# Attention's inverse row sums: spread into the bank of the head outputs, one query tile later

## What is computed

```
o = lax.map(q_block, (qn_b, qr_b, jnp.arange(n_blk)))   # 8 query tiles of 128, 8 heads
  sc = (q_nope . k_nope + q_rope . k_rope) * scale       # block-causal mask, CHUNK = 64
  p  = softmax(sc)
  out = p @ v                                            # 64 columns per head
```

## Time and profile before

| | us |
|---|---|
| median of three executions | 1252.3 |
| lowest, highest | 1246.91, 1253.53 |
| the profiled execution | 1250.46 |
| its span in the profile | 1248.4 |
| attention in it, window 106 to 300.5 | 194.5, of which TensorE busy 184.10, VectorE 127.11, ScalarE 115.39 |

### The profile page before, as it was taken

How to read it: one execution, slowest core, us unless ns; L and a number is a source line. 1 busy time by engine, 2 the same in 40 slices (tenths; PEclk the granted TensorE clock), 3 DMA queues, 4 the chain that set the end, 5 groups by cost and what they waited for, 6 DMA issues and landing times.

```text
span 1248.4 us, 18136 instructions
## 1 busy us (share of the span) xinstructions
PE 1108.9 (89%) x6835; PEld 963.9 (77%) x6835; DVE 712.3 (57%) x832; ACT 564.8 (45%) x756; POOL 327.0 (26%) x276
## 2 busy tenths in 40 slices
PE   3998999999999899999998999329999999999940
PEld 3885888888877788888887888329999999999930
DVE  5874666666055711111114232558888888888838
ACT  5334655655144200000003221407888888888823
POOL 3103222212332223333220000122444444444210
PEclk9988999999999999999999999659999999999975
DMA  7010000021204111111113322537999999999737
GB/s 244 1 28 11 7 7 7 7 69 34 52 1 111 34 34 51 49 37 50 51 51 104 105 75 77 212 121 300 394 368 356 341 348 356 363 379 358 284 141 288
DMA packets 93131, 184.27 MB, mean 148 GB/s; under 512 B 29712, under 2 KB 67088, under 8 KB 79248
## 3 DMA queue, kind: packets, MB, share of 16 engines
q1 hardware_dynamic: 82704, 166.65, 38.4%
q0 software_dynamic: 10368, 16.80, 3.6%
HBM read 177.12 MB, written 27.26 MB: 164 GB/s over the span
## 4 chain that ended last, share of the span: by engine, by line
PE 78%; DVE 11%; ACT 4%; issue 2%; DMA 2%; SPq 1%; POOL 0%; ACTq 0%; POOLq 0%; DVEq 0%
PE ps L369 24%; PE ps L371 23%; PE ps L370 23%; PE ps L858 3%; PE ps L658 2%; DVE pt_lo L1319 1%; PE ps L818 1%; DVE negm L1274 1%; SPq L348 1%; DVE q_tmp L1265 1%; ACT prob L987 1%; DVE acc L1600 1%; DVE res L1610 1%; DVE acc L1601 1%; PE ps L667 1%
## 5 line engine op out<-in xcount | busy, mean ns | idle before, releaser
L1554 DVE TENSOR_TENSOR we_lo<-raw_e,we_hi 128x2048 fp32r<-128x2048 f32 x108 | 246.9, 2288 | 48.3 <-ACT we_hi L1096 48.3
L1096 ACT ACTIVATE we_hi<-raw_e 128x2048 fp32r<-128x2048 f32 x108 | 206.1, 1908 | 8.3 <-DMA raw_e<-in_w_exp_gate_dram 3.7
L369 PE MATMUL ps<-ht_hi,w_hi 128*128 128x512 f32 x448 | 176.4, 394 | 0.4 <-DVE ht_lo L1192 0.4
L371 PE MATMUL ps<-ht_hi,w_lo 128*128 128x512 f32 x448 | 174.7, 390 | 0.0
L370 PE MATMUL ps<-ht_lo,w_hi 128*128 128x512 f32 x448 | 174.6, 390 | 0.0
L369 PE MATMUL ps<-we_hi,xst_hi 128*128 128x256 f32 x576 | 169.4, 294 | 0.0
L370 PE MATMUL ps<-we_lo,xst_hi 128*128 128x256 f32 x576 | 163.5, 284 | 0.0
L371 PE MATMUL ps<-we_hi,xst_lo 128*128 128x256 f32 x576 | 163.4, 284 | 0.0
L363 POOL CAST w_hi<-raw 128x1024 fp32r<-128x1024 f32 x36 | 40.7, 1130 | 302.2 <-PE ps L371 270.3
L369 PEld LDWEIGHTS ps<-we_hi,xst_hi 128*128 128x128 f32 x576 | 111.4, 193 | 0.0
L370 PEld LDWEIGHTS ps<-we_lo,xst_hi 128*128 128x128 f32 x576 | 111.1, 193 | 0.0
(11 more groups left out here) (284 smaller groups left out, 2472.8 us busy)
## 6 DMA issues: line engine op xcount, KB each, us to landing
raw_e<-in_w_exp_gate_dram SPq DMA_DIRECT2D x36, 1024.0 KB, 8.6
raw_e<-in_w_exp_up_dram SPq DMA_DIRECT2D x36, 1024.0 KB, 7.9
raw_e<-in_w_exp_down_dram SPq DMA_DIRECT2D x36, 1024.0 KB, 8.7
raw<-in_w_in_dram SPq DMA_DIRECT2D x27, 512.0 KB, 3.8
yin<-y_dram SPq DMA_DIRECT2D x16, 512.0 KB, 6.6
xin<-in_x_dram SPq DMA_DIRECT2D x8, 512.0 KB, 7.2
raw<-in_w_out_dram SPq DMA_DIRECT2D x8, 512.0 KB, 4.1
xre<-in_x_dram SPq DMA_DIRECT2D x8, 512.0 KB, 4.2
```

The costliest lines, as they stand in the source:

```text
L369: pe.matmul(dst, st[0], mv[0], start=first, stop=False)
L371: return pe.matmul(dst, st[1], mv[0], start=False, stop=last)
L1096: act.activation(we_hi[c % 4][:, :], raw_e[c % 6][:, :], ACT.Copy).then_inc(sem("w_hi_ready"), 1)
L1554: dve.tensor_tensor(we_lo[c % 4][:, :], raw_e[c % 6][:, :], we_hi[c % 4][:, :].bitcast(F32), ALU.subtract).then_inc(sem("w_lo_ready"), 1)
```

## The change

`spread_sums(g)` leaves the rotation and writes bank 6, the bank in which `values` gathers the outputs. Banks 4 and 5 are left to the chunks of probabilities, and the table, `bank_of` and `bank_free` go. In the loop the spread stands one step later, between `scores(s + 2)` and `prob_transposes(s)` of steps 5, 9, 13 and so on, and waits until ScalarE has copied bank 6 (`o_copied`). VectorE's `outputs` moves from the end of a fourth step to the start of the next one, ahead of its `row_max`. `values` of the next group now waits for `o_ready`, VectorE's multiplication, where it waited for `o_copied`. After the loop the last spread follows `values(63)` as before, with the new wait.

```diff
-PASSES = []
-for _s in range(NQ):
-    PASSES += [(0, _c) for _c in range(chunks_through(_s - 1) if _s else 0, chunks_through(_s))]
-    if _s % 4 == 0 and _s:
-        PASSES.append((1, _s // 4 - 1))
-PASSES.append((1, NQ // 4 - 1))
-PASS_OF = {_x: _n for _n, _x in enumerate(PASSES)}
...
-        def bank_of(kind, n):
-            return 4 + PASS_OF[kind, n] % 2
...
-                def bank_free(kind, n):
-
-                    if PASS_OF[kind, n] >= 2:
-                        was, m = PASSES[PASS_OF[kind, n] - 2]
-                        pe.wait_ge(sem("o_ready" if was else "pt_lo_ready"), m + 1)
...
-                        bank_free(0, c0 + c)
+                        if c0 + c >= 2:
+                            pe.wait_ge(sem("pt_lo_ready"), c0 + c - 1)
...
                 def spread_sums(g):
 
                     pe.wait_ge(sem("rl_ready"), g + 1)
-                    bank_free(1, g)
+                    pe.wait_ge(sem("o_copied"), g + 1)
                     for i in range(4):
-                        mm = pe.transpose(ps[:, bank_of(1, g), i * P:(i + 1) * P],
+                        mm = pe.transpose(ps[:, 6, i * P:(i + 1) * P],
...
                     if s and s % 4 == 0:
-                        pe.wait_ge(sem("o_copied"), s // 4)
+                        pe.wait_ge(sem("o_ready"), s // 4)
...
                 for s in range(NQ):
                     if s + 2 < NQ:
                         scores(s + 2)
+                    if s % 4 == 1 and s > 1:
+                        spread_sums(s // 4 - 1)
                     prob_transposes(s)
                     if s:
                         values(s - 1)
-                        if s % 4 == 0:
-                            spread_sums(s // 4 - 1)
...
                     if (s + 1) % 4 == 3:
                         inverse_sums((s + 1) // 4)
+                    if s % 4 == 1 and s > 1:
+                        outputs(s // 4 - 1)
                     if s + 2 < NQ:
                         row_max(s + 2)
...
-                    if s % 4 == 0 and s:
-                        outputs(s // 4 - 1)
                     if i < 4 and h + 1 < HEADS:
                         job_read(h + 1, i)
```

More of the change, by code:

```diff
@@ L655, in prob_transposes @@
                     for c in range(i // 4 + 1):
-                        bank_free(0, c0 + c)
+                        if c0 + c >= 2:
+                            pe.wait_ge(sem("pt_lo_ready"), c0 + c - 1)
                         for j in range(4 * c, min(4 * c + 4, i + 1)):
-                            mm = pe.transpose(ps[:, bank_of(0, c0 + c), (j % 4) * P:(j % 4) * P + P],
+                            mm = pe.transpose(ps[:, 4 + (c0 + c) % 2, (j % 4) * P:(j % 4) * P + P],
                                               prob[s % 2][:, j * P:(j + 1) * P], ident[:, :])
@@ L1012, in _ @@
                             act.wait_ge(sem("pv_done"), used + 1)
-                        act.activation(pt_hi[cc % 4][:, 0:w, :].rearrange("p a b -> p (a b)"), ps[:, bank_of(0, cc), 0:w * P],
+                        act.activation(pt_hi[cc % 4][:, 0:w, :].rearrange("p a b -> p (a b)"), ps[:, 4 + cc % 2, 0:w * P],
                                        ACT.Copy).then_inc(sem("pt_hi_ready"), 1)
@@ L1288, in outputs @@
                     dve.wait_ge(sem("sums_spread"), g + 1)
-                    dve.tensor_tensor(o, ps[r:r + VH, bank_of(1, g), :], o, ALU.mult).then_inc(sem("o_ready"), 1)
+                    dve.tensor_tensor(o, ps[r:r + VH, 6, :], o, ALU.mult).then_inc(sem("o_ready"), 1)
                 for t in range(1, NT, 2):
@@ L1318, in _ @@
                         dve.wait_ge(sem("pt_hi_ready"), cc + 1)
-                        dve.tensor_tensor(pt_lo[cc % 4][:, 0:w, :].rearrange("p a b -> p (a b)"), ps[:, bank_of(0, cc), 0:w * P],
+                        dve.tensor_tensor(pt_lo[cc % 4][:, 0:w, :].rearrange("p a b -> p (a b)"), ps[:, 4 + cc % 2, 0:w * P],
                                           pt_hi[cc % 4][:, 0:w, :].rearrange("p a b -> p (a b)").bitcast(F32), ALU.subtract).then_inc(sem("pt_lo_ready"), 1)
-                    if s % 4 == 0 and s:
-                        outputs(s // 4 - 1)
                     if i < 4 and h + 1 < HEADS:
```

## The result

Thirteen executions of each kernel on one chip gave a median of 1254.34 us with the change and 1250.87 us before it. The measured ratio is 1.0035, with a 95% interval of 1.0018 to 1.0052: the change makes the kernel 2.3 to 6.5 us longer (the two medians are 3.5 us apart). The forecast was 4.9 us longer and 1257 us. The median of 1254.34 us lies inside the range, and the cause was named; the size of one term was off. Of the 2.9 us between 1257.2 and 1254.34, 1.4 us come from the kernel before, whose median over thirteen executions is 1250.87 us and not the 1252.3 us of the three on which the forecast was put.

What follows compares the result with a forecast made beforehand. TensorE, 78% of the chain, was taken to bound the kernel. Head places 3.2, last head place 1.12 and end 0.93, less 0.3 at half-head places, made 4.9 us longer: 1257 us from the 1252.3 median, range 1250 to 1262.

Steps and rivals of the forecast that it cites:

- Half-head places: Eight places: the spread's removed 5.4 us of waits worth about nothing, as the next row maximum starts at the same moment.
- Even and odd heads: Half-head places: row maximum overlaps the multiplication by 0.07 us in even heads, nothing taken in odd; 0.3 us gained.
- some 11 us in all: Forecast total of the values' fifteen waits for the multiplication in the list of PE's waits after the change.
- Head places with a job: Six places: values wait 1.00 us for the multiplication, 0.47 given back by the scores' slack; 3.2 us lost in all.
- Last head place and end: Last head place without a job loses 1.12 us; after the last values, spread and stage U lose 0.93 us.
- Nothing is given back: Rival, chance 0.20: at head places all of the 1.00 us counts; 7.8 us longer, 1260.1 us.
- The removed wait pays: Rival, chance 0.13: half-head places gain up to 0.85 us each; 1.6 us less, 1250.7 us.
- Nothing at all: Rival, chance 0.10: losses lie ahead of stages that would wait later anyway; 1252.3 us stays.

Runs made afterwards that it cites:

- half_b7_new: half_only with the spread in bank 7 instead of bank 6, so values wait for the copy; distances 11.48 and 11.74 us, loop 177.45 us.
- half_b7_maxfirst: half_b7_new with VectorE's row maximum ahead of the multiplication; distances 10.95 and 11.20 us, loop 4.5 us less than before the change.
- half_only: The change at the eight half-head places alone, against the kernel before; distances 11.48, 11.74 and 12.78 us, loop 177.45 us against 177.78.
- no_end: The whole change, but the last spread as before it, in banks 4 and 5; stage U starts 0.17 us after the last output copy.
- head_only: The change at the seven head places alone, against the kernel before; distances 13.16 and 9.31 us, median 1256.54 against 1251.45 us, ratio 1.0029.
- head_rot_new: head_only with the spread kept in the rotation of banks 4 and 5; distances 12.37 us at six places, 8.59 us at the last.
- half_b7_old: Kernel before, with only the half-head places' spread moved to bank 7, order unchanged; distances 10.75 and 10.87 us, loop 171.02 us, 6.8 us less.

## Why the prediction was right, step by step

- **Half-head places: right in mechanism and size.** The row maximum was to start at the same moment and the stretch to keep its length. It kept it to 0.01 us where counted above, the bank made no difference (half_b7_new), and VectorE's order made 4.2 us of difference (half_b7_maxfirst, 173.24 us for the loop against 177.45). TensorE's new wait is 146.39 - (145.28 + 0.61) = 0.50 us by starts, where I had 0.58 and gave 0.4 to 0.6; the transposes ahead of it started a little late, 0.47 us behind the spread's start (144.81, 145.28) where I had 0.37. As said, that wait costs nothing. The list of waits has 0.29 us for it, as it counts past the modelled end. There my own figures were mixed up: the rows give 149.61 - (148.42 + 0.85) = 0.34 us past the modelled end at a half-head place and 162.00 - (160.82 + 0.42) = 0.76 us at a head place, not 0.85 (measured 0.73). So the "some 11 us in all" was a sum by starts and couldn't appear in the list, which has 7.4 us for the fifteen waits.
- **Even and odd heads: right.** The forecast took 0.07 us for even heads and nothing for odd ones; measured are 0.11 us saved and 0.02 us lost, 0.33 us over the loop (half_only) against 0.3. The rows on which it rested were those of an odd head. In even heads the list of waits before the change has no wait of the transposes for `pt_lo`, but the timeline has it: 0.21 us by starts in head 0 (mask 126.83, transposes 127.08), 0.33 us in head 1 (151.20, 151.57). So the row maximum ended the stretch in both. In head 1 the row maximum starts 0.04 us after the multiplication ends (146.24, 146.28). In head 0 it starts 0.07 us before that (120.92 + 0.68 = 121.60, 121.53):

```profile
120.92 0.68 DVE L1270 TENSOR_TENSOR o_t<-ps,o_t 64x512 f32<-64x512 f32 x1 [1.34 <-PE ps L648]
121.53 1.21 DVE L1255 TENSOR_REDUCE negm<-ps 128x1 f32<-128x1024 f32 x1
```

The rule of the Trainium skill ("VectorE: DVE Perf Modes", "Two Vector instructions with no wait between them") agrees with both: the overlap is gone where the PSUM input changes from partition 64 to partition 0. In those heads the output changes from partition 64 to 0 as well (`o_t`, then `negm`), which by the same section is enough to hold an instruction, so these runs don't show which of the two did it.
- **Head places with a job: the mechanism right, the size too large.** This is the mis-sized term: 0.53 us forecast, 0.39 us measured, 0.8 us too much over six. The wait itself was right: the spread's old slot to the values is 3.75 us (162.00 - 158.25) by the forecast and 158.81 - 155.06 = 3.75 us in the trace. Within it, the part given back was too small: 0.47 us forecast, from the scores' start alone, and 1.00 - 0.39 = 0.61 us measured. A part of the rest can be placed. Before, the second scores matmul came 0.30 us after the first:

```profile
162.42 0.47 PE L369 MATMUL ps<-k_hi,q_hi 128*128 128x512 f32 x1 [0.31 <-ACT prob L987]
162.72 0.40 PE L370 MATMUL ps<-k_lo,q_hi 128*128 128x512 f32 x1
```

With the change it comes 0.23 us after (159.72, 159.95), which gives 0.07 us. The wait ahead isn't the reason by itself: before the change there are 0.30 us between two such matmuls with no wait too, where the short values matmuls stand ahead of them (164.23, 164.53), and 0.23 us where a matmul of 512 columns stands right ahead, as it does at 159.72. The job behind the three values starts 0.21 us after them (158.81, 159.02) where it took 0.25 us (161.00, 161.25); that gives 0.04 us. It lies between the first two values matmuls, 0.14 us apart where they stand right behind transposes (161.00, 161.14) and 0.09 us behind the wait (158.81, 158.90). Why is not shown in either case, and the last 0.03 us I can't place.
- **Last head place and end: right to 0.01 us**, 1.12 and 0.93 us (9.31 - 8.19, 1.11 - 0.18). Run no_end takes the second away alone.
- **The rivals.** *Nothing is given back* would have been 13.77 at head places; measured 13.16. The rule on rotating banks from the Trainium skill ("Perfetto Trace Analysis", "Matmuls") holds at the head places, where the same order gives a distance of 13.16 us with the outputs' bank and 12.37 us in the rotation (head_only, head_rot_new), and makes no difference at the half-head places, where half_only and half_b7_new are alike to 0.01 us. *The removed wait pays* is refuted for the change, yet half_b7_old shows that the wait was worth its full 0.85 us: it was not hidden, it was handed to VectorE's order. *Nothing at all* falls by the interval.

## What to carry to other kernels

A wait taken from one engine pays only if what it released isn't released later by a second engine's order: write down the new start of each engine's next instruction, and look for one that stays where it was. A step that reads or writes a shared buffer belongs behind the work that others wait for (here the multiplication behind row maximum and `pt_lo`), and into a buffer that stands idle at that place, found place by place; the same edit cost at one kind of place and was free at another. A last or first round without its usual neighbour (no job to cover the copy) needs its own line in the sum: two of sixteen places made half of this loss.

## What the runs showed of the hardware

The same code ahead of attention took 4.2 us less in the profile after than in the one before, most of it by the clock that TensorE was granted. The first transposes of the probabilities start at 108.5 us before and at 104.3 us after, where nothing differs between the kernels (first and last start of all instructions of the line):

```profile
L658 PE MATMUL ps<-ident,prob x288: 272/273/455, 108.5 to 296.6; 128*128 128x128 f32 x144
```

```profile
L639 PE MATMUL ps<-ident,prob x288: 272/273/455, 104.3 to 296.2; 128*128 128x128 f32 x144
```

By stages (us, busy times, then the mean granted clock ahead of the last two columns), before and after:

```profile
75.00:105.00 30.00, 26.89 (x110) 20.23 (x108) 14.65 (x25) 10.61 (x22) 4.28 (x4) 0.82 0.12 25
660.00:705.00 45.00, 41.76 (x196) 34.63 (x195) 20.53 (x21) 16.82 (x21) 0.00 (x0) 1.00 0.41 121
```

```profile
75.00:105.00 30.00, 24.94 (x117) 18.79 (x115) 15.35 (x27) 12.57 (x27) 7.67 (x9) 0.90 0.11 24
660.00:705.00 45.00, 41.76 (x176) 34.05 (x176) 19.31 (x20) 15.59 (x18) 0.00 (x0) 0.92 0.43 121
```

A mean of 1.00 is 2.4 GHz throughout; one between 0.5 and 1 is a stretch spent partly at 1.2 GHz. The profile before stood there longer ahead of attention (0.82 against 0.90), the one after around 680 us (0.92 against 1.00). Of the 4.2 us, 1.0 us was there at 80 us already (the first matmul with `wv_hi` starts at 81.4 and at 80.4 us), where the clock isn't the reason: the profile before had 1.00 throughout up to there. The other 3.2 us arise between 80 and 95 us, where a matmul of 512 columns follows the one ahead by 0.42 us in the profile before (89.39, 89.81; granted clock 0.72 from 85 to 90 us and 0.60 from 90 to 95) and by 0.23 us in the one after (87.13, 87.36; 1.00 in both). Around 680 us it is the other way: the profile after is 0.9 us behind at the first matmul with `mt_lo` (680.1, 681.0) and 3.2 us behind at the router's first input `h2t` (699.8, 703.0), with a granted clock of 0.77 from 675 to 690 us where the one before had 1.00.

So the difference of the two spans, 3.8 us, is made of three parts: 3.5 us gained up to the first output copy (122.37, 118.88), 4.1 us lost by the change, and 3.2 us lost behind it. The first and the last lie where the code is the same. Single executions of one kernel differ by up to 9 us (1250.04 to 1259.06). The distances of a repeated instruction inside the attention loop, where the granted clock is 1.00, repeat to 0.03 us from one kernel to the next where their code agrees, so one profile shows what the times need many executions for.
